# Tokens loaded ahead of the conditioning slabs, squared as they lie, and the first norm in groups of four rows

## The reference

```python
silu_c, silu_cc = jax.nn.silu(c), jax.nn.silu(c_ctx)[None]
mod_l = jnp.split((silu_c  @ ada_w[i] + ada_b[i])[:, None], 6, axis=-1)
mod_c = jnp.split((silu_cc @ ada_w[i] + ada_b[i])[:, None], 6, axis=-1)
sh_l, sc_l, g_l, sh2_l, sc2_l, g2_l = mod_l
h_lat = rmsnorm(x_lat, norm_w[i, 0]) * (1 + sc_l) + sh_l
h_ctx = rmsnorm(x_ctx, norm_w[i, 0]) * (1 + sc_c) + sh_c
# hgrn2: q, zf, zb, v, g = split(h @ w_in); gates, scans in chunks of 64 tokens, readout
def rmsnorm(x, w):
    return x * lax.rsqrt(jnp.mean(x * x, axis=-1, keepdims=True) + EPS) * w
```

## Time and profile before

| | |
|---|---|
| median of three runs | 2251.61 us (2251.16 to 2253.8) |
| the profiled execution | 2257.25 us, span 2254.3 us |
| TensorE matmul busy | 2126.8 us, 94% of the span |
| VectorE, ScalarE busy | 1091.2 us (48%), 825.8 us (37%) |
| mean granted TensorE clock | 0.970 |
| DMA, mean over the span | 91 GB/s |
| DMA in the first fortieth of the span (56 us) | 270 GB/s |

### The profile page before, as it was taken

The page is one execution under the profiler, slowest core; times in us unless marked ns, Lnnn a source line. Parts: engine busy times, 40 slices in busy tenths (PEclk is TensorE's granted clock), DMA queues, the critical chain, the costliest instruction groups (busy, mean ns, idle before and its releaser), DMA issues.

```text
span 2254.3 us, 33844 instructions
## 1 busy us (share of the span) xinstructions
PE 2126.8 (94%) x13412; PEld 1892.8 (84%) x13412; DVE 1091.2 (48%) x1607; ACT 825.8 (37%) x1278; POOL 50.4 (2%) x79
## 2 busy tenths in 40 slices
PE   5899999999989999999999889999998898999998
PEld 3899999998889999999999867777775687888887
DVE  4755555557452222222234757767676545333334
ACT  2543334334232221122222454737382425532322
POOL 1000000000000000000000100000000000000000
PEclk8999999999989999999999989999999899999999
DMA  7322222213323332233321221221215232332332
GB/s 270 125 76 85 76 85 85 82 60 113 112 75 112 114 98 76 85 112 112 97 77 47 79 57 37 66 64 43 79 47 177 75 94 69 99 109 84 97 102 75
DMA packets 297512, 204.42 MB, mean 91 GB/s; under 512 B 5012, under 2 KB 289037, under 8 KB 295629
## 3 DMA queue, kind: packets, MB, share of 16 engines
q1 hardware_dynamic: 293965, 180.03, 26.4%
q0 software_dynamic: 3456, 23.09, 2.8%
HBM read 189.47 MB, written 13.63 MB: 90 GB/s over the span
## 4 chain that ended last, share of the span: by engine, by line
PE 78%; DVE 11%; ACT 7%; issue 3%; DMA 1%; SPq 0%; ACTq 0%; DVEq 0%; POOL 0%
PE G L309 65%; PE G L415 2%; PE S L1491 1%; ACT whi L292 1%; PE S L765 1%; DVE acc L1522 1%; ACT e L1367 1%; DVE hlo L646 1%; PE S L736 1%; PE S L1487 1%; DVE hn L638 1%; DVE wlo L296 1%; DVE cum L985 1%; PE S L1671 1%; PE G L421 1%
## 5 line engine op out<-in xcount | busy, mean ns | idle before, releaser
L309 PE MATMUL G<-hhi,whi 128*128 128x384 f32 (+2 forms) x2336 | 731.8, 371 | 31.2 <-DVE hlo L646 20.1
L309 PE MATMUL G<-hlo,whi 128*128 128x384 f32 (+2 forms) x2336 | 683.8, 351 | 0.0
L309 PE MATMUL G<-hhi,wlo 128*128 128x384 f32 (+2 forms) x2336 | 683.8, 351 | 0.0
L296 DVE TENSOR_TENSOR wlo<-raw,whi 128x1024 fp32r<-128x1024 f32 (+1 forms) x225 | 288.1, 1281 | 810.4 <-ACT whi L292 810.1
L292 ACT ACTIVATE whi<-raw 128x1024 fp32r<-128x1024 f32 (+1 forms) x225 | 248.7, 1106 | 958.0 <-PE G L309 487.5
L309 PEld LDWEIGHTS G<-hhi,whi 128*128 128x128 f32 x2336 | 425.2, 192 | 99.3 <-issue 36.3
L309 PEld LDWEIGHTS G<-hhi,wlo 128*128 128x128 f32 x2336 | 435.0, 191 | 20.7
L309 PEld LDWEIGHTS G<-hlo,whi 128*128 128x128 f32 x2336 | 435.8, 192 | 18.1
L309 PE MATMUL G<-mhi,whi 128*128 128x384 f32 (+2 forms) x550 | 165.6, 346 | 0.0
L309 PE MATMUL G<-mlo,whi 128*128 128x384 f32 (+2 forms) x550 | 165.2, 345 | 0.0
L309 PE MATMUL G<-mhi,wlo 128*128 128x384 f32 (+2 forms) x550 | 165.2, 345 | 0.0
(11 more groups left out here) (277 smaller groups left out, 2098.4 us busy)
## 6 DMA issues: line engine op xcount, KB each, us to landing
raw<-in_ffn_w_in_dram SPq DMA_DIRECT2D x88, 512.0 KB, 3.7
raw<-in_ffn_w_out_dram SPq DMA_DIRECT2D x32, 704.0 KB, 4.5
raw<-in_ssm_w_in_dram SPq DMA_DIRECT2D x41, 512.0 KB, 3.8
raw<-in_hg_w_in_dram SPq DMA_DIRECT2D x40, 512.0 KB, 3.9
adaw<-in_ada_w_dram SPq DMA_DIRECT2D x20, 1024.0 KB, 6.1
adaf<-in_ada_w_dram SPq DMA_DIRECT2D x20, 1024.0 KB, 5.0
ada<-in_ada_w_dram SPq DMA_DIRECT2D x4, 2048.0 KB, 13.2
raw<-in_ssm_w_out_dram SPq DMA_DIRECT2D x16, 512.0 KB, 3.9
```

Of the source, the lines that this page charges most:

```text
L296: dve.tensor_tensor(wlo[pn.slot][:, 0:kt, :], raw[pn.slot][:, 0:kt, :], f32(whi[pn.slot][:, 0:kt, :]), ALU.subtract).then_inc(s["lo"], 1)
L309: ins = pe.matmul(G[:, tl.slot, g0:g0 + n], w[pn.slot][:, k, :], r[:, k_base + k, t0:t0 + n], start=(first and k == 0 and i == 0), stop=(l ...
```

## The change

The tokens are loaded before the slabs, each block with a semaphore of its own. ScalarE squares a block as it lies, with tokens on the partitions (`sqx`), and VectorE reduces it to a column (`xsum`), between the copies to `x0`. The mean of all blocks is made at once, and the sum over partitions by TensorE is gone. The first two slabs loaded are now 2 and 0, that is scale and shift of rows 0 to 3; their buffers lie in the space of `hhi` and `hlo`. Slabs 3 and 1 (rows 4 to 7) come behind the first two weight panels, in `ada0` and `ada1`. The first norm takes rows 0 to 3 of both halves of the tokens, then rows 4 to 7 of both. `product_pair` is replaced for this norm by `product_first`, in which TensorE also does the strips and turns of the last two slabs; ScalarE copies their rows, and VectorE waits for the turned columns before steps 7 and 8.

```diff
+    for w in ("hi", "lo"):
+        run(m_at["h" + w], (f"ada{w}", (P, KT, 512)))
...
+        def norm_place(N, v):
+            return (v // KT, v % KT) if N else (v % KT // 4, v // KT * 4 + v % 4)
...
+        SLABS = (2, 0, 3, 1)
+        ada, arow = (m["adahi"], m["adalo"], m["ada0"], m["ada1"]), (m["arow0"], m["arow1"])
...
+        def slab_strips(pe, i):
+            pe.wait_ge(s[f"slab{i}"], 16)
+            strips(pe, [(S[:, i % 2, :], ada[i])]).then_inc(s["ada"], 1)
...
+        def product_first(pe, pn):
+            product_begin(pe, pn, pn)
+            for u in range(2 * KT + LAG):
+                if u < 2 * KT:
+                    e, k = norm_place(0, u)
+                    pe.wait_ge(s["hlo"], u + 1)
+                    ins = product_block(pe, pn, pn, m["hhi"], m["hlo"], k, KT, SEGS, half=e, apart=False)
+                if u == 2 * KT - 1:
+                    product_end(pe, pn, ins, rows=0)
+                if u == LAG:
+                    product_begin(pe, pn + 1, pn + 1)
+                if u >= LAG:
+                    e, k = norm_place(0, u - LAG)
+                    ins = product_block(pe, pn + 1, pn + 1, m["hhi"], m["hlo"], k, KT, SEGS, half=e, apart=False)
+                if u == 2:
+                    slab_strips(pe, 2)
+                if u == 4:
+                    slab_strips(pe, 3)
+                if u == 5:
+                    pe.wait_ge(s["arows"], 1)
+                    slab_turned_of(pe, 2)
+                if u == 7:
+                    pe.wait_ge(s["arows"], 2)
+                    slab_turned_of(pe, 3)
+            product_end(pe, pn + 1, ins, turn=m["mrow0"])
+
+        def first_rows(act, v):
+            if v in (5, 7):
+                i = (v - 5) // 2
+                act.wait_ge(s["ada"], 5 + i)
+                act.activation(arow[i][:, :], S[:, i, :], ACT.Copy).then_inc(s["arows"], 1)
+
+        def first_mods(dve, v):
+            if v in (7, 8):
+                dve.wait_ge(s["ada"], v)
+                slab_mods(dve, v - 5)
+            if v == 8:
+                dve.wait_ge(s["modev"], 6)
+                factors(dve, 0, 0, 4, KT)
...
-            for n in (0, 1):
-                slab_sync(sp, n)
             for b in range(NBLK):
...
-            for n in (2, 3):
-                slab_sync(sp, n)
+            for i in (0, 1):
+                slab_sync(sp, i)
+            for j, kind in ((0, QUERY), (1, FWD)):
+                load_panel(sp, At(j), cols_of(hg_w_in[0], HG_OFF[kind]), KT)
+            for i in (2, 3):
+                slab_sync(sp, i)
...
+            rsqrt_pool(pool, 0, NBLK)
             pool.wait_ge(s["x"], NBLK * 2)
+            pool.wait_ge(s["hn"], KT + 1)
             pool.dma_start(x_park0, m["x0"][:, :, :]).then_inc(s["parked0"], 16)
...
+            for b in range(NBLK):
+                act.wait_ge(s[f"xin{b}"], 16)
+                if b >= 2:
+                    act.wait_ge(s["sqd"], b - 1)
+                act.activation(m[f"sqx{b % 2}"][:, :], m["xin"][:, b, :], ACT.Square).then_inc(s["sq"], 1)
...
+            for b in range(NBLK):
+                for q in (0, 1):
+                    u = 2 * b + q
+                    dve.wait_ge(s["xt"], u + 1)
+                    dve.tensor_copy(m["x0"][:, 4 * q:4 * q + 4, b * P:(b + 1) * P],
+                                    Gq[:, u % 4, :].rearrange("p (j t) -> p j t", j=4)).then_inc(s["x"], 1)
+                dve.wait_ge(s["sq"], b + 1)
+                dve.tensor_reduce(m["xsum"][:, b:b + 1], m[f"sqx{b % 2}"][:, :], axis=mybir.AxisListType.X,
+                                  op=ALU.add).then_inc(s["sqd"], 1)
...
+            for i in (0, 1):
+                slab_strips(pe, i)
+            for i in (0, 1):
+                pe.wait_ge(s["modev"], i + 1)
+                slab_turned_of(pe, i)
+            pe.wait_ge(s["ps"], N_CONST)
+            pe.wait_ge(s["modev"], 4)
+            pe.wait_ge(s["rstd"], 1)
+            # ... six matmuls that spread rstd, for both halves
```

More of the change, by code:

```diff
@@ L176, in memory @@
                ("act0", (P, T)), ("mid0", (P, T)), ("mrow1", (P, SLAB)), ("adaf", (P, KT, SLAB))) <= N
-    run(m_at["xin"], *[(f"{n}a{i}", (P, T)) for n in ("sq", "hn") for i in (0, 1)])
+    run(m_at["xin"], *[(f"hna{i}", (P, T)) for i in (0, 1)])
     run(m_at["mlo"], ("sqb0", (P, T)), ("sqb1", (P, T)), ("sumb", (P, T)))
@@ L790, in hg_tensor @@
             if h is None:
-                product_pair(pe, 0, pn, pn, SEGS, rows=0, turn=m["mrow0"])
+                product_first(pe, pn)
             for j in range(3 if h is None else 0, 5):
@@ L1154, in ffn_sync @@
             ffn_loop(sp, gate_up, down, last, l)
-        ada, arow = (m["ada0"], m["ada1"]), (m["arow0"], m["arow1"])
-        def slab_sync(sp, n):
-            if n >= 2:
-                sp.wait_ge(s["ada"], n - 1)
-            sp.dma_start(ada[n % 2][:, :, :], ada_w[0][:, n * 512:(n + 1) * 512].rearrange("(k p) n -> p k n", p=P))\
-                .then_inc(s[f"slab{n % 2}"], 16)
-        def slabs_tensor(pe, pair):
-            for n in (0, 1):
-                pe.wait_ge(s[f"slab{n}"], 16 * (pair + 1))
-                if pair:
-                    pe.wait_ge(s["modev"], 4)
-                strips(pe, [(S[:, n, :], ada[n])]).then_inc(s["ada"], 1)
-            for n in (0, 1):
-                pe.wait_ge(s["modev"], 4 * pair + n + 1)
-                for b in range(4):
-                    ins = turned(pe, S[:, 2 + n, 2 * b:2 * b + 2], block(arow[n][:, :], b))
-                ins.then_inc(s["ada"], 1)
@@ new lines, in slab_turned_of, with slab_mods @@
+        def slab_turned_of(pe, i):
+            for b in range(4):
+                ins = turned(pe, slab_columns(i)[:, 2 * b:2 * b + 2], block(arow[i % 2][:, :], b))
+            ins.then_inc(s["ada"], 1)
+        def slab_mods(dve, i):
+            t = SLABS[i] * 4
+            bias = m["colB"][:, t:t + 4].rearrange("p (t a) -> p t a", a=1)
+            dve.tensor_tensor(m["mods"][:, 0, t:t + 4, :], slab_columns(i).rearrange("p (t a) -> p t a", a=2),
+                              bias.to_broadcast([P, 4, 2]), ALU.add).then_inc(s["modev"], 1)
@@ L2099, in _ @@
                 ins.then_inc(s["xt"], 1)
[L2100 removed]
+            pe.wait_ge(s["cols"], 2)
+            pe.wait_ge(s["csil"], 1)
+            pe.wait_ge(s["ps"], N_PICK)
+            for i in (0, 1):
+                slab_strips(pe, i)
+            for i in (0, 1):
+                pe.wait_ge(s["modev"], i + 1)
+                slab_turned_of(pe, i)
             pe.wait_ge(s["ps"], N_CONST)
[L2102 removed]
+            pe.wait_ge(s["modev"], 4)
+            pe.wait_ge(s["rstd"], 1)
             for e in (0, 1):
[L2104 to L2106 removed]
+                b0 = half_blocks(SEGS, e).start
+                for b in half_blocks(SEGS, e):
+                    ins = pe.matmul(block(factors_of(SEGS, e), b - b0), m["rstd"][:, b:b + 1].to_broadcast([P, P]),
+                                    ident[:, :], start=True, stop=True)
+                ins.then_inc(s["rbc"], 1)
             hg_all(pe, lambda *a: hg_tensor(pe, *a))
```

128 lines of the change are left out of this document (52 added, 76 removed).

## The result

The changed kernel takes 2240.57 us, the median of 5 runs (2238.73 to 2243.56). The kernel before, run beside it, takes 2252.33 (5 runs, 2251.16 to 2253.8). The ratio is 0.9949, with a 95% interval of 0.9935 to 0.9964: 11.8 us faster, or half a per cent. The forecast was 2238.2, in a range of 2233.5 to 2244.0. The profiled execution took 2240.57 us with a span of 2238.8; its mean granted clock is 0.974, against 0.970 before.

What follows compares the result with a forecast made beforehand. A chain of waits to the first normalised row at 55.15 (tokens behind slabs, then serial squares, sums and slabs), then VectorE, bounded it. Last hlo 14.4 us earlier minus 1.0 for slab_rows gave 13.4: 2251.61 to 2238.2, range 2233.5 to 2244.0.

Steps and rivals of the forecast that it cites:

- The loads: Opening loads: same bytes, tokens first at 0.41 MB/us; slabs land at 20.2, 25.3, 33.4 and 38.5.
- The token stage: VectorE's copies and reduction per block, 2.45 us each, done at 24.2 under the second slab's load, costing nothing.
- A: Opening, chance 0.46: first slab's strips slow, second's fast; first normalised row at 32.3, total 2238.2 us.
- s: Start of the first normalised row: 55.15 before, forecast 32.3, 22.8 us earlier.
- B: Opening, chance 0.26: second slab's strips and turns at half clock; first normalised row at 35.7, total 2241.6 us.
- The stop: Between the norm's two eights, VectorE waits 3.8 and 2.3 us for TensorE's turns; cost 8.5 us.
- Were it at half clock again after the wait, it still catches up before u = 15.: TensorE behind the second turn: two blocks take 2.0 against rows 1.18 to 1.43 apart, for about 4 us.
- slab_rows at the end: End of the first pair: moved before the count ACT awaits, it makes whi 1.0 us later against the last hlo.
- The operations for lb, the memsets and x_park0: Behind the norm on VectorE, 2.65 us, hidden; x_park0 lands at 62.7, awaited at 65.0, hidden by 2.3 us.
- C: Norm, chance 0.14: wait between the eights half hidden by earlier strips on TensorE; total 2233 to 2234 us.
- D: First pair, chance 0.06: TensorE stays at half clock throughout, so the total shows no change.
- E: Late loads, chance 0.03: fourth slab lands late, at 61.9 on the slowest rate; 6.6 us slower, 2258.

Runs made afterwards that it cites:

- e2: Changed kernel with the third slab's strips ahead of the first block and the fourth's behind u = 2, turns and row copies earlier; 2236.92 us, ratio 0.9930.
- e7: Changed kernel with late slabs' strips moved earlier, both turns behind u = 3, VectorE taking both mods only before the ninth row; 2233.35 us, ratio 0.9911.
- e4: Changed kernel with all four slabs turned ahead of the norm, rows in the old order of eights, old pair; 2241.87 us, ratio 0.9957.
- e1: Changed kernel without strips, turns and copies of the last two slabs, reusing scale and shift of rows 0 to 3; 2233.35 us, ratio 0.9913.
- e3: Changed kernel with half of slab_rows' small matmuls done at u = 11, the other half at the end; 2242.58 us, ratio 0.9950.
- e9: e4 with the first two slabs loaded and turned ahead of the tokens, as before the change; 2243.85 us, ratio 0.9958.
- e6_before_tokens_first: Kernel before the change with only the token loads moved ahead of the first two slabs; 2247.05 us, ratio 0.9972.
- e8_all: Changed kernel with the edits of e7 and e3, plus the first slab's strips computed twice; 2234.64 us, ratio 0.9912.

## Why the prediction was nearly right

The sum was 13.4 us and the medians give 11.8; at the third panel's whi it is 11.3. Step by step:

- **The loads.** Forecast: slabs at 20.2 and 25.3. Read: strips begin at 20.06 and 25.14. Right; the rate of 0.41 MB/us read from the earlier trace rows carries over to another order of the same bytes. The late slabs were forecast at 33.4 and 38.5. In the changed kernel TensorE comes to them later and waits for neither; where a kernel did wait, the third began at 33.62 (e2) and 34.22 (e7), the fourth at 40.96 (e7).
- **The token stage.** 2.45 us a block and done at 24.2 were forecast; it is one block in 2.32 and done at 24.0. The reduction of 1024 columns takes 1.21, the upper of the two bounds. It costs nothing, as said: it isn't on the chain.
- **The chain to the first row.** Here A (s = 32.3) and B (35.7) were the cases. s is 33.28, between them: the second strips take 3.53, as in B, after a pause of 3.18 us, but the clock is back before the turns, which take 1.97 and not the 3.58 that B had. B was made of two terms that I tied together, and only one of them came. A had the right size with the wrong picture: it had the first strips slow and the second fast, and here it is the other way round. In the executions of other kernels with this same start the first strips took 3.3 to 3.5 and the second 1.90 (e2, e4, e7), or 1.90 and 3.4 to 3.5 (e1, e3). With the first s was 31.91 and 32.47 (e2, e7), with the second 33.28 to 34.48 (the changed kernel, e3 and e1). So it is in part luck that the profiled s lies as near to A as it does.
- **The stop.** This is the term that was mis-sized: 8.5 forecast, 9.6 measured (e1_no_stop). Of the two waits the first was right, 4.04 for 3.8. The second is 3.85 where 2.3 stood. The blocks u = 6 and 7 were priced at full clock; in the trace TensorE falls to half at about 49.2, 0.7 us after it has taken up work behind the pause from 46.9 to 48.46, so twelve products take 3.65 us, and the turn behind them 1.27 instead of 0.95.
- **"Were it at half clock again after the wait, it still catches up before u = 15."** It does, at about 63.5, but with nothing to spare, and e3_half_rows shows that no work can be hidden there.
- **slab_rows at the end.** Forecast +1.0. From the last hlo to whi there were 1.80 us (75.99 to 77.79) and are now 2.82: 1.0. e1_no_stop has s + 23.6 against s + 22.6 before, and e4 and e9, with `slab_rows` in the old place, have 1.80 and 1.79. Right.
- **The operations for lb, the memsets and x_park0.** whi waits for none of them, and wlo of the third panel, which stands behind the wait for x_park0, starts at 67.71 and is put down to whi. x_park0 is issued at 54.84 (0.73) and lands 10.9 us later, by 66.5 at the latest; VectorE comes to its wait at 64.45 + 2.65 = 67.1. The cover is then at least 0.6 us, less than the 2.3 forecast: the landing took 0.9 more than in the earlier trace rows, and the issue came 1.2 after the ninth row's start, not 0.6.

At the third panel's whi the changed kernel is 2.1 us behind the forecast: 1.0 in s, 1.1 in the stop. In both the term that was too small is work of TensorE at half clock behind a pause. C (the stop half hidden) was not the case, but its reason, that the program's places and not the loads hold the late strips back, is what e2 and e7 confirm, up to the last 3 us: with the places moved the times are 2236.92 and 2233.35, the second of which lies in C's range. D and E did not come: the clock did rise in the pair, and the last slab's strips (43.0) waited for no load.

Still open: what decides whether the first strips run slow. Where they do, they end later, and the pause before the second group is short (1.75 us in e2_early_strips, 1.72 in e7_late_mods) and the second runs at 1.90; where they don't, the pause is 3.1 to 3.2 and the second runs slow. Both were seen with the same start. Why the clock falls in the spread of rstd, with no pause ahead of it, wasn't tried. In the total, kernels whose whi differs by 1 to 2 us were not told apart from each other, and e6_before_tokens_first gained 6.3 us between medians with 4.2 at the third panel; where the other 2 are from is open. The median execution of the kernel before had a mean granted clock of 0.972 in that comparison and that of e6 0.974, so a part may be the clock further on. The spread of single executions, some 5 us, is as large.

## What to carry to other kernels

A stage that starts on half of its inputs pays twice: once for the stop where the other half is needed, and again if the engine that prepares it loses its clock in the pause. Count what the stop costs before the earlier start is taken as a gain, and place the late half's work so that it is done when the consumer comes, with each wait at the first true use; here that was 6.6 us of 9.6. And what brought the gain was work taken under a load that had to be awaited anyway, on the data as they lie.

## What the runs showed of the hardware

- In the changed kernel the granted clock went from 1.00 to 0.50 behind pauses of 3.18, 1.56 and 2.41 us, 0.1 to 0.7 us after work was taken up again; the last two had only turns of two columns a matmul just ahead of them. It also fell at 32.1, in the middle of a spread behind turns, with no pause longer than 0.30 us. Other pauses left it at full: 1.46 in e7_late_mods, 1.60 before 36.24 in e4_four_slabs_first, 2.45 in e8_all. So the length of the pause alone doesn't tell.
- The same 16 strips took 1.90 to 3.6 us, and in the opening either the first or the second group was slow, from one execution to the next.
- The first slab's strips began at 20.06 to 21.11 in kernels whose queue is the same up to there: a spread of 1 us in 20 of loading.
- While ScalarE squared and VectorE reduced the blocks, the load ran at 403 to 409 GB/s (stretches of 8 us between 8 and 24); the kernel before, without that work, had 408 to 424 between 8 and 22. So the work under the load cost the load little, if anything.
- Between executions of one kernel the time goes with the mean granted clock: 2250.32 us at 0.973 and 2256.03 at 0.970 for the kernel before, 2239.46 at 0.974 and 2247.64 at 0.971 for e3_half_rows. One execution of e9 stands apart, 2243.63 at 0.929.
